# Attention keys scaled by -1/sqrt(96), and minima of negated scores as biases of the exponentials

## The reference

```python
q = (c_q @ w_uq).reshape(B, S, 16, 96)            # 64 plain, 32 rotary
kv = (c_kv @ w_ukv).reshape(B, S, 16, 128)        # 64 key, 64 value columns
scale = 96 ** -0.5
s = (q_nope @ k_nope.T + q_rope @ k_rope.T) * scale
s = where(key_pos <= q_pos, s, -inf)
o = softmax(s) @ v                                # per head
mix = o.reshape(B, S, 1024) @ w_o
```

## Time and profile before

| | us |
|---|---|
| median of 3 runs | 1304.67 |
| lowest, highest run | 1304.33, 1304.68 |
| profiled execution | 1304.9 |
| its span, first to last instruction | 1303.1 |
| TensorE busy in the span | 1298.2 |
| VectorE, ScalarE, GpSimd busy | 649.2, 287.8, 86.9 |

### The profile page before, as it was taken

The page is one execution under the profiler, slowest core; times in us unless marked ns, Lnnn a source line. Parts: engine busy times, 40 slices in busy tenths (PEclk is TensorE's granted clock), DMA queues, the critical chain, the costliest instruction groups (busy, mean ns, idle before and its releaser), DMA issues.

```text
span 1303.1 us, 25215 instructions
## 1 busy us (share of the span) xinstructions
PE 1298.2 (100%) x10760; PEld 852.5 (65%) x10760; DVE 649.2 (50%) x1471; ACT 287.8 (22%) x432; POOL 86.9 (7%) x116
## 2 busy tenths in 40 slices
PE   9999999999999999999999999999999999999998
PEld 5878888888997444555555555555555555555555
DVE  5888666666887344233433533423343353342436
ACT  4874444433694000010010010001001001000102
POOL 3401111111002110000000000000000000000100
PEclk9999999999999999999999999999999999999999
DMA  8625555556369999999999999999999999999992
GB/s 304 253 105 173 193 192 193 193 193 210 120 249 378 358 416 406 421 409 414 419 408 416 419 420 405 419 419 405 405 420 410 403 420 421 411 413 419 419 411 101
DMA packets 124423, 441.92 MB, mean 339 GB/s; under 512 B 7346, under 2 KB 18052, under 8 KB 109732
## 3 DMA queue, kind: packets, MB, share of 16 engines
q1 hardware_dynamic: 119696, 424.57, 82.5%
q0 software_dynamic: 4560, 15.85, 3.4%
q10 hardware_dynamic: 68, 0.02, 0.0%
HBM read 430.84 MB, written 9.57 MB: 338 GB/s over the span
## 4 chain that ended last, share of the span: by engine, by line
PE 98%; ACT 1%; DMA 1%; SPq 0%; issue 0%; DVE 0%
PE psum L1663 67%; PE psum L441 9%; PE psum L443 8%; PE psum L442 8%; PE psum L1210 1%; PE psum L1669 1%; DMA raw<-in_mla_w_in 1%; PE psum L1317 0%; ACT w_hi L412 0%; PE psum L1305 0%; PE psum L1326 0%; PE psum L1341 0%; PE psum L1316 0%; PE psum L1615 0%; PE psum L1428 0%; PE psum L457 0%
## 5 line engine op out<-in xcount | busy, mean ns | idle before, releaser
L1663 PE MATMUL psum<-raw_more,hT 128*32 128x512 f32 x1656 | 535.7, 592 | 0.0
L1663 PE MATMUL psum<-raw,hT 128*32 128x512 f32 x1032 | 334.6, 592 | 0.0
L1663 PE MATMUL psum<-raw_more,xg_odd 128*32 128x512 f32 x1680 | 245.4, 592 | 0.0
L1663 PE MATMUL psum<-raw_more,xg 128*32 128x512 f32 x1704 | 241.8, 592 | 0.1
L2473 DVE STREAM_TRANSPOSE hT<-hid 32x128 f32<-32x128 f32 x672 | 206.2, 307 | 10.3
L2463 DVE SCALAR_TENSOR_TENSOR hid<-hid,psum 96x512 f32<-96x512 f32 x55 | 37.6, 683 | 302.7 <-PE psum L1663 301.9
L1154 ACT ACTIVATE hid<-psum 96x1024 f32<-96x1024 f32 (+1 forms) x32 | 29.2, 914 | 663.8 <-PE psum L1663 474.2
L1663 PEld LDWEIGHTS psum<-raw_more,hT 128*32 128x32 f32 x1656 | 154.3, 110 | 32.0 <-issue 32.0
L1663 PEld LDWEIGHTS psum<-raw_more,xg_odd 128*32 128x32 f32 x1680 | 84.5, 110 | 98.0 <-issue 98.0
L1663 PEld LDWEIGHTS psum<-raw_more,xg 128*32 128x32 f32 x1704 | 83.4, 110 | 98.2 <-issue 97.8
L1663 PE MATMUL psum<-raw,xg_odd 128*32 128x512 f32 x1008 | 147.7, 592 | 0.0
(11 more groups left out here) (368 smaller groups left out, 1352.6 us busy)
## 6 DMA issues: line engine op xcount, KB each, us to landing
raw_more<-in_moe_w_gate SPq DMA_DIRECT2D x71, 1024.0 KB, 18.4
raw_more<-in_moe_w_up SPq DMA_DIRECT2D x70, 1024.0 KB, 18.6
raw_more<-in_moe_w_down SPq DMA_DIRECT2D x69, 1024.0 KB, 17.7
raw<-in_moe_w_down SPq DMA_DIRECT2D x43, 1024.0 KB, 18.0
raw<-in_moe_w_up SPq DMA_DIRECT2D x42, 1024.0 KB, 17.5
raw<-in_moe_w_gate SPq DMA_DIRECT2D x41, 1024.0 KB, 18.3
raw<-in_ffn_w_gate SPq DMA_DIRECT2D x14, 1024.0 KB, 5.2
raw<-in_ffn_w_up SPq DMA_DIRECT2D x14, 1024.0 KB, 5.3
```

The source lines that it names most:

```text
L1663: return pe.matmul(psum[rows_q, bank, cols], stationary, moving, start=start, stop=stop, tile_position=(0, rows_q.start), skip_group_check ...
```

## The change

The keys are stored multiplied by -SCALE, all 96 columns of them: ScalarE's and VectorE's key copies and GpSimd's copies of the rotary columns become multiplies by a constant. TensorE's scores are then the negated, scaled ones. The mask holds +3e38 above the diagonal. VectorE takes minima in place of maxima, and they are the biases themselves; L2047 and the waits between the reductions go, and `max_ready` is raised after each of the two reductions, so it counts two per head. ScalarE's exponentials have scale -1.0, and each waits for its own reduction.

```diff
@@ gpsimd
             pool.affine_select(out=mask[:, P:2 * P], in_=mask[:, P:2 * P], compare_op=ALU.is_ge,
-                               fill=-BIG, base=0, pattern=[[-1, P]], channel_multiplier=1).then_inc(const, 1)
+                               fill=BIG, base=0, pattern=[[-1, P]], channel_multiplier=1).then_inc(const, 1)
...
-                pool.tensor_copy(k[:, t, :, NOPE:QK],
-                                 latent[:, t, QR + KVR:LAT].unsqueeze(1).broadcast_to([P, HEADS, ROPE])
-                                 ).then_inc(qk_ready, 1)
+                pool.tensor_scalar(k[:, t, :, NOPE:QK],
+                                   latent[:, t, QR + KVR:LAT].unsqueeze(1).broadcast_to([P, HEADS, ROPE]),
+                                   -SCALE, None, ALU.mult).then_inc(qk_ready, 1)
@@ scalar
-                copy(k[:, t, 4 * b:4 * b + 4, 0:NOPE], src[:, :, 0:NOPE]).then_inc(kv_copied_a, 1)
+                act.activation(k[:, t, 4 * b:4 * b + 4, 0:NOPE], src[:, :, 0:NOPE], ACT.Copy,
+                               scale=-SCALE).then_inc(kv_copied_a, 1)
...
-                act.wait_ge(max_ready, h + 1)
                 b = h % 4
                 for r, (c0, c1) in enumerate([(0, P), (P, 3 * P)]):
-                    act.activation(probs[:, b, c0:c1], probs[:, b, c0:c1], ACT.Exp, scale=SCALE,
+                    act.wait_ge(max_ready, 2 * h + r + 1)
+                    act.activation(probs[:, b, c0:c1], probs[:, b, c0:c1], ACT.Exp, scale=-1.0,
@@ tensor
                 if h >= 2:
-                    pe.wait_ge(max_ready, h - 1)
+                    pe.wait_ge(max_ready, 2 * (h - 1))
@@ vector
-                dve.tensor_copy(k[:, t, 4 * b:4 * b + 4, 0:NOPE], src[:, :, 0:NOPE]).then_inc(kv_copied_v, 1)
+                dve.tensor_scalar(k[:, t, 4 * b:4 * b + 4, 0:NOPE], src[:, :, 0:NOPE], -SCALE, None,
+                                  ALU.mult).then_inc(kv_copied_v, 1)
...
                 for r, (c0, c1) in enumerate([(0, P), (P, 3 * P)]):
-                    link(dve.tensor_tensor_reduce(probs[:, b, c0:c1], psum[:, 2 + h % 2, c0:c1],
-                                                  mask[:, 2 * P - (c1 - c0):2 * P], 1.0,
-                                                  -BIG, ALU.add, ALU.max, mx[:, 2 * b + r:2 * b + r + 1]))
-                dve.tensor_scalar(nmx[:, 2 * b:2 * b + 2], mx[:, 2 * b:2 * b + 2], -SCALE, None,
-                                  ALU.mult).then_inc(max_ready, 1)
+                    dve.tensor_tensor_reduce(probs[:, b, c0:c1], psum[:, 2 + h % 2, c0:c1],
+                                             mask[:, 2 * P - (c1 - c0):2 * P], 1.0,
+                                             BIG, ALU.add, ALU.min,
+                                             nmx[:, 2 * b + r:2 * b + r + 1]).then_inc(max_ready, 1)
```

More of the change, by code:

```diff
@@ L184, in trunk @@
         att = res_row[:, 12 * P:13 * P].rearrange("p (a b) -> p a b", b=32)
-        mx, nmx, tot, inv = att[:, 0], att[:, 1], att[:, 2], att[:, 3]
+        nmx, tot, inv = att[:, 1], att[:, 2], att[:, 3]
         Q_BANKS = [(4, 5, 2), (6, 7, 3)]
```

## The result

The changed kernel takes 1307.93 us (median of 15 runs, 1307.06 to 1308.68) against 1304.67 us of the kernel before in the same comparison (15 runs, 1304.14 to 1305.35). The ratio is 1.0024, with a 95% interval of 1.0016 to 1.0031: 3.3 us slower, just outside the 0.2% that had been called no change. The forecast was 1304.7 with a range up to 1306.0.

What follows compares the result with a forecast made beforehand. The prediction took TensorE to bound the kernel; VectorE 0, ScalarE 0 and GpSimd 0 left the profiled 1304.9 us, and the runs' median lying 0.2 us lower gave 1304.7 us, range 1303.9 to 1306.0.

Steps and rivals of the forecast that it cites:

- The bound: Whole kernel: TensorE has work in 1298.2 of 1303.1 us, so only what removes or delays its work counts.
- The two cushions: Before the first attention matmuls: 0.3 us behind GpSimd's copies plus about 0.55 us of ScalarE stalls, 0.85 us in all.
- VectorE: Per head, multiply and waits gone: about 2.4 us off its queue, worth 0 to the end, at most -0.5 us.
- ScalarE: Exponentials, with a separate wait for each head's second one: cost taken as 0, at most +0.8 us.
- the key copies: Six on ScalarE and two on VectorE, now multiplying by a constant: cost taken as 0 for both.
- I take 0.8, nearest to the copy: GpSimd's rotary key multiplies: 0.8 us each, the pair ending about 0.1 us later, so 0 at the end.
- The upper bound, 1.4: GpSimd's rotary key multiplies: at most 1.4 us each, of which +0.45 us would reach the end.
- The step behind it: At GpSimd's second key multiply: VectorE's last rotary product would be held up, so the multiply would precede the split.
- rival 3: At GpSimd's rotary key multiplies: one is held up behind a VectorE split, +1.6 us, 1306.3 us; chance 5%.
- a split's 2.70 us: VectorE's split beside GpSimd's second copy took 2.70 instead of 2.28 us, read as agreeing with mutual exclusion.
- Rival 4: At GpSimd's rotary key multiplies: both are held up at 2.7 to 2.8 us, +3.2 us, 1308.1 us; chance 3%.

Runs made afterwards that it cites:

- work for TensorE: The changed kernel with 36 matmuls of zeros in TensorE's queue where it waits for GpSimd's key multiplies: 1306.73 us, ratio 1.0017.
- plain copies: The changed kernel with GpSimd's two key multiplies put back to copies, leaving the rotary key columns unscaled: 1304.51 us, ratio 1.0001.
- the narrow multiply in front: The changed kernel, but GpSimd scales the 2x32 rotary key columns once, right before two unscaled copies to the heads: 1306.25 us, ratio 1.0014.
- the late splits: The changed kernel with one wait more: VectorE starts two splits of output weights only after GpSimd's key multiplies: 1306.61 us, ratio 1.0015.

## Why the prediction was wrong

**The bound, right.** TensorE is the bound, and what reaches it in the attention reaches the end. The two cushions existed: the distance between the copies and the first weight load, and the stalls on ScalarE. In the run with the multiplies kept apart from the clock (work for TensorE), the first transposes start 2.50 us later than with plain copies (49.17 and 46.67) and the feed-forward's input 2.09 later (100.78 and 98.69), so the stalls gave back 0.41 us; I had 0.55.

**VectorE, ScalarE, the key copies: right.** All were costed at nothing, and together they measure 1.0001 of the kernel before (0.9992 to 1.001). That minima are no slower than maxima, which the forecast took for granted, is in the rows.

**The step that failed: "I take 0.8, nearest to the copy, which has the same single input and the same shape."** The multiply's own length is 1.50 to 1.57 us. The upper bound, 1.4, was worked out from a two-input product per element and was nearly right; I rejected it for a likeness in shape. The page GPSIMD Engine Reference of the Trainium skill (section 3.1) gives 769 ns for 512 elements in its best case, without naming an operation. The copy agrees (0.72 us on average); the multiply, which has one input as well, takes twice that.

**The step behind it, the argument against rival 3: VectorE's last rotary product "would itself be held up by the first multiply, so the second is in line before the split".** It was not held that long. In the changed kernel this product runs from 44.95 to 45.67 and takes 0.72 us, as beside the copies (0.42 in the run with the narrow multiply in front), while the multiply runs from 44.73 to 46.29. The first split then starts at 45.59, inside the same multiply, and takes 2.28 us all the same. The second multiply starts at 46.37, when that split has 1.5 us to go, and takes 2.87 us for 1.5. The trace of before could have shown it: there, too, the product (45.43, 0.72 us) is over while the copies still run. The page SBUF — State Buffer of the Trainium skill (section SBUF: two separate sides) has the pair exclude each other for the whole of the first one's length. The trace agrees for a GpSimd instruction that comes behind a split: the split ends at 47.87, and the multiply 1.37 us later, at 49.24. It does not agree for VectorE's instructions that come behind a GpSimd one, neither for this product, which both began and ended inside the multiply, nor for the split at 45.59; a split's 2.70 us in the earlier trace rows, which the prediction gave as the rule's sign, did not come back there. Here the longer GpSimd instruction did not keep its successor's place in the row; it lost it.

**What was missing altogether: the clock.** No rival had a stall of TensorE cost more than its length. After a gap of 2.44 us the granted clock stood at 0.51 for 3.4 us, 1.2 to 1.55 us more. After gaps of 1.0 and 1.6 us (the runs with the late splits and with the narrow multiply in front) it was 1.00, and the matmuls kept their distance of 0.23 us.

**The sum, put together again,** in profiles, against the run with plain copies: first transposes 2.62 us late (46.67 to 49.29), of which some 1.3 is the two multiplies' own excess beyond the cushion, and some 1.3 the split beside the second; 1.59 us slower to the second head's (1.84 and 3.43 us); 0.44 us given back by the stalls; 3.77 us at the feed-forward's input (98.69 and 102.46). The medians, 1304.51 and 1307.93, lie 3.4 us apart, and the profiled execution of the changed kernel is one of its slower ones (1308.54). Rival 3 had the mechanism with one multiply held up and 1306.3; the multiply's length and the clock, which it lacked, make up the difference. Rival 4's time of 1308.1 was near, but only by luck: its mechanism, both held up, is not what happened, and its sum should read 1307.9 (1304.7 + 3.2), as the other rivals start from 1304.7.

## What to carry to other kernels

An instruction that only changes its operation on GpSimd is a change of length, and its length decides what stands beside it next: look in the trace at which VectorE product or split will start before the next instruction on GpSimd, and price that one with its neighbour's length. Scale or convert before data is spread, in a stretch where the engine is waiting anyway. And price a new gap of TensorE twice, for its own length and for the matmuls behind it at the lower clock; where the gap can't go, cheap matmuls in it save the second part.

## What the runs showed of the hardware that was not expected

- A multiply by a constant on GpSimd, 128x512 in float32, takes 1.50 to 1.57 us where the copy of the same operands takes 0.7 to 0.8; the 128x64 one takes 0.44 us at one place and 0.81 at another.
- A GpSimd copy that starts 0.5 us behind a VectorE split takes 2.67 us instead of 0.8. The other way round, a VectorE product of 0.72 us ran from start to end inside a GpSimd multiply, and a split that started inside one took 2.28 us, the mean of its group in the earlier trace rows.
- TensorE idle for 2.4 us was followed by 3.4 us at a granted clock of 0.51; with 36 matmuls of zeros in the same wait it stayed at 1.00.
- One wait more on VectorE, on a semaphore raised long before, made the kernel 1.1 us slower, in its last output transfer (3.4 us to land instead of 2.4). In the two profiles with the long transfer, and in no other, a fetch of instructions falls among its last packets; that this is the cause is argued, not shown. It also means that, in a kernel timed to 0.1%, an experiment that adds an instruction needs such a run beside it.
